# Hybrid attention layer: v's weights gathered on the host and loaded in four pieces, three x loads on ACT's queue, an early table load, and the later heads' second key copy made by DMA

## The reference

```python
h = rmsnorm(x, pre_g)
p = jnp.einsum('btd,de->bte', h, w_in)
aq, ak, av, ag, bq, bk, bv, bg = split_projection(p)   # widths 512,128,128,512,512,512,512,512
ya = sliding_window_sink_attention(aq, ak, av, sinks) * jax.nn.silu(ag)
# group B: 4 heads, each with two query/key maps (n = 0, 1) of 64 and one value of 128,
# swept in blocks of 128 queries (blocks 0 to 7)
s = jnp.einsum('bqhnd,bshnd->bhnqs', qs, ks) * scale   # plus ALiBi, chunk-causal mask
p = jax.nn.softmax(s, axis=-1)
attn = p[:, :, 0] - lam * p[:, :, 1]
o = jnp.einsum('bhqs,bshe->bqhe', attn, vs)
yb = rmsnorm(o, subln_g) * (1.0 - lambda_init) * jax.nn.silu(bg)
y = jnp.einsum('bte,ed->btd', jnp.concatenate([ya, yb], axis=-1), w_out)
return x + rmsnorm(y, post_g)
```

## Time and profile before

| what | value |
|---|---|
| median of 3 runs | 515.28 us (515.09 to 517.2) |
| profiled execution, own time | 516.69 us |
| its span, first to last instruction | 514.9 us |
| PE busy | 502.5 us (98%) |
| DVE busy | 283.8 us (55%) |
| ACT busy | 260.0 us (50%) |
| POOL busy | 105.3 us (20%) |
| chain that ended last | PE 85%, DVE 5%, ACT 4%, issue 3%, DMA 2%, POOL 1% |

### The profile page before, as it was taken

The page is one execution under the profiler, slowest core; times in us unless marked ns, Lnnn a source line. Parts: engine busy times, 40 slices in busy tenths (PEclk is TensorE's granted clock), DMA queues, the critical chain, the costliest instruction groups (busy, mean ns, idle before and its releaser), DMA issues.

```text
span 514.9 us, 7476 instructions
## 1 busy us (share of the span) xinstructions
PE 502.5 (98%) x2724; PEld 422.0 (82%) x2724; DVE 283.8 (55%) x676; ACT 260.0 (50%) x622; POOL 105.3 (20%) x139
## 2 busy tenths in 40 slices
PE   8999999999999999999999999999999999999995
PEld 8999987888877888888887777688788888888884
DVE  4959734555557545545457687554663593433332
ACT  7932543556575557656577766633644471222211
POOL 1070503223032021213043335212303000000000
PEclk9999999999999999999999999999999999999998
DMA  8810042020111010110002010111000834322221
GB/s 313 266 46 0 2 121 81 12 71 0 42 43 24 19 41 1 42 41 17 26 1 74 10 42 0 43 43 41 1 0 1 193 136 148 126 95 83 81 92 72
DMA packets 41540, 32.05 MB, mean 62 GB/s; under 512 B 18784, under 2 KB 36128, under 8 KB 41504
## 3 DMA queue, kind: packets, MB, share of 16 engines
q1 hardware_dynamic: 38912, 26.85, 18.2%
q10 hardware_dynamic: 2592, 4.72, 2.5%
HBM read 26.88 MB, written 4.19 MB: 60 GB/s over the span
## 4 chain that ended last, share of the span: by engine, by line
PE 85%; DVE 5%; ACT 4%; issue 3%; DMA 2%; POOL 1%; SPq 0%; DVEq 0%; POOLq 0%; ACTq 0%
PE proj L1212 39%; PE scores L1318 15%; PE scores L1143 8%; PE scores L1233 6%; PE banks L1254 6%; PE banks L1244 3%; PE scores L1279 2%; DVE k_stack L993 2%; PE proj L1143 1%; PE banks L1143 1%; PE banks L1299 1%; PE banks L1287 1%; DMA w_raw<-in_w_in 1%; DVE a_weights L1079 1%; ACT weights L801 1%
## 5 line engine op out<-in xcount | busy, mean ns | idle before, releaser
L645 POOL TENSOR_TENSOR w_lo<-w_raw,w_hi 128x256 fp32r<-128x256 f32 x84 | 62.9, 779 | 170.4 <-ACT w_hi L726 170.4
L1212 PE MATMUL proj<-hT_hi,w_hi 128*128 128x512 f32 x336 | 89.9, 400 | 1.4 <-DVE q_stack L988 0.8
L1212 PE MATMUL proj<-hT_hi,w_lo 128*128 128x512 f32 x336 | 89.5, 401 | 0.0
L1212 PE MATMUL proj<-hT_lo,w_hi 128*128 128x512 f32 x336 | 88.5, 400 | 0.0
L1048 DVE CUSTOM_DVE_ANT_0 weights<-scores,dist_b 128x128 f32<-128x128 f32 (+7 forms) x64 | 45.9, 754 | 53.9 <-PE scores L1233 53.7
L1212 PEld LDWEIGHTS proj<-hT_hi,w_hi 128*128 128x128 f32 x336 | 60.6, 188 | 14.6 <-DVE q_stack L988 1.2
L1212 PEld LDWEIGHTS proj<-hT_hi,w_lo 128*128 128x128 f32 x336 | 60.6, 188 | 13.3 <-issue 1.9
L1212 PEld LDWEIGHTS proj<-hT_lo,w_hi 128*128 128x128 f32 x336 | 60.6, 188 | 11.9 <-issue 0.8
L801 ACT ACTIVATE weights<-weights,small 128x128 f32<-128x128 f32 (+7 forms) x64 | 49.0, 767 | 15.1 <-DVE small L1048 15.1
L811 ACT ACTIVATE weightsT<-banks 128x512 f32<-128x512 f32 (+3 forms) x48 | 23.6, 491 | 56.1 <-PE banks L1244 56.0
L1233 PE MATMUL scores<-k_stack,q_stack 128*128 128x512 f32 (+3 forms) x192 | 41.8, 353 | 0.0
(11 more groups left out here) (125 smaller groups left out, 749.3 us busy)
## 6 DMA issues: line engine op xcount, KB each, us to landing
w_raw<-in_w_in SPq DMA_DIRECT2D x13, 512.0 KB, 3.8
w_raw<-in_w_in SPq DMA_DIRECT2D x16, 256.0 KB, 3.7
x_res<-in_x SPq DMA_DIRECT2D x8, 512.0 KB, 4.4
out<-y_out ACTq DMA_DIRECT2D x16, 256.0 KB, 2.3
x_all<-in_xT SPq DMA_DIRECT2D x7, 512.0 KB, 7.1
wo_raw<-in_w_out SPq DMA_DIRECT2D x8, 256.0 KB, 5.3
wo_raw<-in_w_out SPq DMA_DIRECT2D x4, 512.0 KB, 9.1
wv_raw<-in_w_in SPq DMA_DIRECT2D x8, 160.0 KB, 6.6
```

Source lines behind the costliest of these rows:

```text
L645: nc.gpsimd.tensor_tensor(w_lo[:, n % SPLIT, k], w_raw[:, n % RAW, k], w_hi[:, n % SPLIT, k].bitcast(F32), ALU.subtract).then_inc(w_lo_rea ...
L1212: last = nc.tensor.matmul(to, w[:, slot, k, :], h[:, k, HALF * half:HALF * half + HALF], start=(p == 0 and k == first), stop=(p == PIECES ...
```

## The change

The host hands over v's weights as an own array `wv`, laid out as [128 rows, 2 groups, 8 k, 320], so that several k of one group are one contiguous run for each row. SP's queue then carries: gains, `wv` of k = 0, the second half of slab 0, `wv` of k = 1 to 3, x of 2, x of 4, `wv` of k = 4 to 7... in the order of the diff, and last the whole of group 1. ACT's queue carries the first half of slab 0 and the slabs 1 and 3. ACT then copies `ones` to `junk`, which loads its table before x is needed. There are seven warm-up products instead of eight. For the heads 1 to 3, ACT and DVE write only the rows of the map itself, and SP copies both parts to the other rows by two DMAs for each half (`move_k`), behind a wait for DVE's writes; PE waits for these copies (`k_moved`) ahead of every `b_scores` of those heads. Head 0 is as before.

```diff
-WARM_UP = 8
+WARM_UP = 7
+V_LOADS = [slice(0, 1), slice(1, 4), slice(4, KT)]
...
-        parts = [2 if UNITS[m][0] == "qB" else 4 for m in STACKED]
+        parts = [4 if UNITS[m] == ("kB", 0) else 2 for m in STACKED]
...
+            def load_wv(i):
+                k = V_LOADS[i]
+                sp.dma_start(wv_raw[:, 0, k, :], wv[:, 0, k, :]).then_inc(wv_loaded[i], 16)
+
             sp.dma_start(g_column, g_columns[:, :]).then_inc(g_loaded, 16)
-            for k in range(KT):
-                if k:
-                    sp.dma_start(x_all[:, k, :], x_slabs[:, k, :]).then_inc(x_loaded[k + 1], 16)
-                sp.dma_start(wv_raw[:, 0, k, :], w_cols[:, k, BV:BV + VG]).then_inc(wv_loaded[k], 16)
-            for i, (first, count, to) in enumerate(v_runs):
-                sp.dma_start(wv_raw[:, 1, :, to:to + count],
-                             w_cols[:, :, first:first + count]).then_inc(wv_loaded[KT + i], 16)
+            load_wv(0)
+            sp.dma_start(x_all[:, 0, HALF:SEQ], x_slabs[:, 0, HALF:SEQ]).then_inc(x_loaded[1], 16)
+            load_wv(1)
+            load_x(2)
+            load_x(4)
+            load_wv(2)
+            for k in range(5, KT):
+                load_x(k)
+            sp.dma_start(wv_raw[:, 1, :, :], wv[:, 1, :, :]).then_inc(wv_loaded[3], 16)
...
-            for n in range(2, NU):
+            def move_k(n, half):
+
+                tokens = slice(HALF * half, HALF * half + HALF)
+                sp.wait_ge(stack_lo, stack_count(n, half))
+                for m in range(2):
+                    own, other = (slice(HEAD_DIM * e, HEAD_DIM * (e + 1)) for e in (m, 1 - m))
+                    sp.dma_start(k_stack[other, :, m, tokens].bitcast(F32),
+                                 k_stack[own, :, m, tokens].bitcast(F32)).then_inc(k_moved[half], 16)
+
+            for n in range(2, 2 + RAW):
                 load_w(n)
+            for step, *i in SCHEDULE:
+                if step == "low" and i[1] == LOWS - 1 and i[0] + RAW < NU:
+                    load_w(i[0] + RAW)
+                elif step == "store_low" and UNITS[i[0]][0] == "kB" and UNITS[i[0]][1]:
+                    move_k(*i)
...
-            for part, tokens in enumerate(token_parts(0)):
-                act.dma_start(x_all[:, 0, tokens], x_slabs[:, 0, tokens]).then_inc(x_loaded[part], 16)
+            act.dma_start(x_all[:, 0, 0:HALF], x_slabs[:, 0, 0:HALF]).then_inc(x_loaded[0], 16)
+            for k in (1, 3):
+                act.dma_start(x_all[:, k, :], x_slabs[:, k, :]).then_inc(x_loaded[k + 1], 16)
+            act.wait_ge(ones_made, 1)
+            nc.scalar.activation(junk[:, :], ones[:, :], ACT.Copy).then_inc(table_loaded, 1)
             act.wait_ge(g_loaded, 16)
...
-                            for part in (own, slice(HEAD_DIM * (1 - m), HEAD_DIM * (2 - m))):
+                            other = slice(HEAD_DIM * (1 - m), HEAD_DIM * (2 - m))
+                            for part in (own,) if head else (own, other):
                                 nc.scalar.activation(k_hi[part, m, tokens], source[own, :],
...
-                            for part in (own, other):
+                            for part in (own,) if head else (own, other):
                                 nc.vector.tensor_tensor(k_lo[part, m, tokens], source[own, :],
...
+                    if head:
+                        for half in range(block_ // 4 + 1):
+                            pe.wait_ge(k_moved[half], 32 * head)
```

More of the change, by code:

```diff
@@ L238, with hybrid_layer @@
 SCHEDULE = make_schedule()
-def hybrid_layer(nc, x, xT, w_in, w_out, g_columns, post_norm_g, sinks, lambda_q1, lambda_k1,
+def hybrid_layer(nc, x, xT, wv, w_in, w_out, g_columns, post_norm_g, sinks, lambda_q1, lambda_k1,
                  lambda_q2, lambda_k2, subln_g, out):
@@ L356, in hybrid_layer @@
     x_loaded = [sem(f"x_loaded{i}") for i in range(KT + 1)]
-    wv_loaded = [sem(f"wv_loaded{i}") for i in range(KT + 2)]
+    wv_loaded = [sem(f"wv_loaded{i}") for i in range(4)]
     w_loaded = [sem(f"w_loaded{i}") for i in range(RAW)]
@@ L361, in hybrid_layer @@
     ones_made = sem("ones_made")
+    table_loaded = sem("table_loaded")
     wv_first = sem("wv_first")
@@ L399, in hybrid_layer @@
     stack_lo = sem("stack_lo")
+    k_moved = [sem("k_moved0"), sem("k_moved1")]
     tanh_done = sem("tanh_done")
@@ L569, in load_count @@
         return sum(16 * len(unit_columns(m)) for m in range(n % RAW, n + 1, RAW))
-    v_runs = [(BV + VG, B_WIDTH - VG, 0), (AV, P, B_WIDTH - VG)]
     x_slabs = xT.rearrange("(k p) t -> p k t", p=P)
@@ L577, in _, with load_x @@
         def _(sp):
[L578 to L585 removed]
+            def load_x(k):
+                sp.dma_start(x_all[:, k, :], x_slabs[:, k, :]).then_inc(x_loaded[k + 1], 16)
+            def load_wv(i):
+                k = V_LOADS[i]
+                sp.dma_start(wv_raw[:, 0, k, :], wv[:, 0, k, :]).then_inc(wv_loaded[i], 16)
+            sp.dma_start(g_column, g_columns[:, :]).then_inc(g_loaded, 16)
+            load_wv(0)
[7 more added lines that the diff above has]
+            sp.dma_start(wv_raw[:, 1, :, :], wv[:, 1, :, :]).then_inc(wv_loaded[3], 16)
             def load_small():
@@ L733, in _ @@
                 if k:
-                    act.wait_ge(wv_loaded[k], 16)
+                    act.wait_ge(wv_loaded[1 if k < V_LOADS[1].stop else 2], 16)
                     nc.scalar.activation(wv_hi[:, 0, k], wv_raw[:, 0, k], ACT.Copy).then_inc(wv_hi_ready, 1)
                 square_x(k)
-            for i in range(2):
-                act.wait_ge(wv_loaded[KT + i], 16)
+            act.wait_ge(wv_loaded[3], 16)
             for part in range(KT // 2):
@@ L1320, in _ @@
                     last.then_inc(out_projected, 1)
-INPUTS = ["x", "xT", "w_in", "w_out", "g_columns", "post_norm_g", "sinks", "lambda_q1", "lambda_k1",
+INPUTS = ["x", "xT", "wv", "w_in", "w_out", "g_columns", "post_norm_g", "sinks", "lambda_q1", "lambda_k1",
           "lambda_q2", "lambda_k2", "subln_g"]
@@ L1334 @@
     laid["xT"] = np.asarray(inputs["x"])[0].T
+    w_rows = np.asarray(inputs["w_in"])[0].reshape(KT, P, -1)
+    v_columns = np.concatenate([w_rows[:, :, BV:BV + B_WIDTH], w_rows[:, :, AV:AV + P]], axis=2)
+    laid["wv"] = v_columns.reshape(KT, P, 2, VG).transpose(1, 2, 0, 3)
     laid["g_columns"] = np.asarray(inputs["pre_norm_g"]).reshape(KT, P).T
```

## The result

The changed kernel takes 516.75 us (median of 20 runs, 516.17 to 518.75), the one before 515.43 us (20 runs, 514.73 to 517.2): 1.3 us more. The ratio on record, which weighs the runs and not the two medians alone, is 1.0019 with an interval of 1.001 to 1.0028 (1.0 us, 0.5 to 1.4), so it is slower by little, but not by nothing. The forecast was 515.2 us and no change.

What follows compares the result with a forecast made beforehand. PE, busy 98% of the span, was taken to bound the kernel. Span 514.9 + 0.5 (start) - 0.6 (keys) = 514.8 us, profiled execution 516.6, median 1.4 lower: 515.2 us, no measurable change; range 513.3 to 517.2.

Steps and rivals of the forecast that it cites:

- the start, put at +0.5 us: Start: slab 0's late second half stalls PE about 0.7 us before the fifth matmul; +0.5 us for the whole start.
- The estimate: Start: summed DMA rates put the landing of slab 0's second half between 6.4 and 7.1 us, 6.75 in the middle.
- The first weights were put at 5.35: Start: k = 0's weights land 0.25 us later than 5.1 beside ACT's bigger loads; PE starts at about 5.8.
- one turn at most: Start: by the skill's queue rule, a bigger neighbour costs the first weights one turn at most, so PE starts at 5.5.
- the prediction's own signs of being wrong: PE starting before 5.2 or having all slab 0 in time, clock rise over 2 us from 9.7, any `b_scores` awaiting DMA.
- the third rival: Start: wait for x's half interrupts PE and delays the clock's rise; +1.55 us there, 516.2 us in all; chance 0.17.
- The median of the runs was 1.4 us under that execution: Whole kernel: profiled execution forecast at 516.6 us, median 1.4 us under it, giving 515.2 us.
- The keys, put at -0.6 us: Head 1: relieved ACT and DVE finish the key stack before PE wants the bank, removing its 0.60 us wait; -0.6 us.
- At heads 2 and 3 PE didn't wait: 0: Keys of heads 2 and 3: PE had no wait for the key stack there, so the gain is 0.
- The fourth rival: Head 1: key copies land 5.8 us after issue, delaying `b_scores` by 1.2 us; 516.4 us in all; chance 0.06.
- The added waits in PE's stream: Heads 1 to 3: 36 added waits cost nothing visible; at 0.02 us each 0.7 us, the upper end.
- The first and second rivals: Start: first, it gets shorter, 514.2 us, chance 0.28; second, PE's clock also rises before real work, 512.7 us, chance 0.07.

Runs made afterwards that it cites:

- e2: The changed kernel with heads 1 to 3's keys written by ACT and DVE as before, leaving the start's part alone: 518.38 us, ratio 1.0058 to the kernel before.
- e12: The kernel before with seven warm-up products instead of eight and nothing else: 516.26 us, ratio 1.0011.
- e9: The kernel before with the keys' part alone, only the high half copied by DMA, DVE still writing both low copies: 514.57 us, ratio 0.9988.
- e1: The kernel before with the keys' part of the change alone (copies by DMA for heads 1 to 3): 513.29 us, ratio 0.9962.
- e4: The kernel before with ten warm-up products instead of eight: 515.08 us, ratio 0.9991.
- e7: The kernel before with the keys by DMA, the early table load and ten warm-up products, start loads as before: 512.98 us, ratio 0.9952.
- e8: e7 with the gathered weights in four loads, in the order of before: 512.92 us, ratio 0.9951 to the kernel before.
- e11: The changed kernel with slab 0's second half back on ACT's queue and ten warm-up products instead of seven: 514.38 us, ratio 0.9976 to the kernel before.
- e6: The changed kernel with twelve warm-up products instead of seven: 515.16 us, ratio 0.9995 to the kernel before.

## Why the prediction was wrong

**The step that failed is the start, put at +0.5 us and worth +3.1 by the medians (+2.0 between the profiled executions).** "I take +0.5 us for the whole start" had the mechanism right (the half of slab 0 third on SP's queue, a new wait ahead of the fifth matmul) and three things too small or missing.

First, the landing. The estimate added up the mean rate of all DMA engines and came to 6.75. A load is there when the slowest engine has done its part. The sixteen parts of this one arrived from 6.28 to 8.07 us: their mean, 6.9, is about where the estimate was, the last 1.3 us behind it. The first weights were put at 5.35 and landed at 6.0 for the same reason: the mean of their sixteen parts moved from 4.45 to 4.70 us, by the 0.25 us that was forecast, the last from 5.1 to 6.0. The start at 5.5 that "one turn at most" was to give didn't follow from it either: if each of the sixteen moves a sixteenth of 303 to 377 GB/s, the neighbour's 8 runs of 4 KB take it 1.4 to 1.7 us, and 8 runs of 2 KB half of that (an estimate from these rates). So a bigger neighbour costs some 0.8 us by turns too, and the landing of 6.0 can't tell turns from sharing. The rate itself was right, 377 and 400 GB/s at 5 to 7 us:

```profile
3.00:5.00 2.00, 1.33 (x7) 1.03 (x5) 0.00 (x0) 1.44 (x3) 0.00 (x0) 1.00 0.93 303
5.00:6.00 1.00, 0.00 (x0) 0.00 (x0) 0.00 (x0) 0.00 (x0) 0.00 (x0) 1.00 1.01 377
6.00:7.00 1.00, 0.60 (x2) 0.61 (x3) 0.95 (x3) 0.00 (x0) 0.00 (x0) 1.00 1.02 400
```

These rows show the failure at its plainest: DMA at its full share, and from 5 to 6 us not one engine of the core at work.

Second, the clock. The forecast let the rise stay at 9.7 or move with the delay; it was 12.5 in the profiled execution, 2.8 us later. More than 2 us was one of the prediction's own signs of being wrong. It looks like the third rival, given 0.17: the wait interrupts the stretch at 1.2 GHz and the rise comes about 4 us behind its end (8.87 to 12.5; 3.6 us). That rival priced itself at 1.55 us, for a landing at 7.1 and not at 8.07. Its mechanism isn't shown: in e2 the wait ended at 7.85 and the rise came at 9.8, 2.0 us behind. That one execution had a landing as forecast and a rise as forecast, and its span is 0.4 us above that of before, about the +0.5 us put for the start.

Third, and this decides the sign: the conversion from the profiled execution to the median. "The median of the runs was 1.4 us under that execution", and I carried this over as a constant. It was no constant but the clock: the profiled execution was one with the late rise, and by their times over half of the other runs had the early one. None of the changed kernel's 20 runs stands below the others as that group did, so none seems to have had the early rise; only one of them was traced. Its median is 0.3 us above its profiled execution and not 1.4 below. Whether the idle time of 2.1 us instead of 0.9 behind the warm-up products did this isn't shown, and neither is what the eighth of them is worth (e12).

Between the two profiled executions the forecast was -0.1 us and the measurement -0.2. That is luck: the start was 1.5 us dearer there than forecast, and the keys paid about 1.5 us more. In the medians the two terms are +3.1 and -2.0 us, errors of 2.6 and 1.4 us, and don't cancel.

The Trainium skill, TensorE: Matmul & The Clock Gate, Part 1, says that the same kernel shows a different number of slow matmuls from run to run. The trace agrees: 15 slow matmuls in the profiled execution of before, none from the first real one on in e9's, with the same start. The Trainium skill also says there that the number of slow matmuls isn't to be fitted, and puts the penalty of the ramp under 1% of a typical kernel's span. Here the two groups of before are 1.6 us or 0.3% apart, which agrees, and is yet more than the whole effect of the change.

**The keys, put at -0.6 us, were worth -2.0.** At head 1 the mechanism was as described, and the copies landed with 0.7 us to spare where the sum had 0.9. "At heads 2 and 3 PE didn't wait: 0" was wrong for head 3: I looked for waits on `k_stack` and not for waits on what stands behind the key writes in DVE's and ACT's order. The fourth rival did not happen.

**The other points.** The table load ran at 2.12 as forecast, the high part was done at 4.8 (4.4 to 4.5 forecast; x's first half landed 0.5 us later than before), and bought nothing, since the weights were the other arm: right. PE's start at 6.4 lies outside the 5.5 to 6.1 that were given. The added waits in PE's stream cost nothing that shows: e1's PE waits for no copy. The first and second rivals were wrong.

## What to carry to other kernels

At a kernel's start order the loads by when the first consumer can use them, across the queues together, and reckon a landing by its slowest DMA engine: a large load on a second queue delays a small one on the first. Keep PE working until its first real matmul (with ten products, in e4, e7, e8 and e11, each kernel's runs lay in one group, 35 in all; with twelve and late loads, in e6, 3 of 12 still stood apart), and look at the runs one by one before taking one profile for the median. When an engine is relieved, look at what stands behind the removed instructions in its order, not only at who waits for their output.

## What the runs showed that was not expected

Two more warm-up products (0.85 us of work on ones) took the kernel from two groups of runs, 1.6 us apart, to one: 11 of 11 runs in e4, 6 of 6 in e7. In e9 and e12 the clock was up behind an idle stretch of 1.0 and 1.5 us: the last warm-up products started 0.21 us apart as at 1.2 GHz (0.11 at 2.4 in e6), the first real matmuls 0.15 us apart. SBUF to SBUF copies of 256 KB for 64 rows took 3.2 to 4.5 us from issue to landing in the changed kernel, and 12 of them beside the unit weights disturbed nothing that PE waited for.
